# One matmul of 512 columns for the high weights in the feed-forward, its halves added when the bank is emptied

## The reference

```python
def conv_ffn(x, w_gate, w_val, conv_w, conv_b, w_down):
    h = causal_dwconv(x @ w_gate, conv_w) + conv_b     # 3 taps over the tokens
    return (jax.nn.silu(h) * (x @ w_val)) @ w_down

x = layer_norm(ALPHA * x + mixers[layer](x), *ln1[layer])
x = layer_norm(ALPHA * x + conv_ffn(x, *ffns[layer]), *ln2[layer])
```

## Time and profile before

| what | value |
| --- | --- |
| median of 3 runs | 3589.15 us (3586.17 to 3608.59) |
| span of the profiled execution | 3590.3 us, 68886 instructions |
| TensorE busy | 3425.7 us, 95% |
| VectorE busy | 2281.9 us, 64% |
| ScalarE busy | 1603.8 us, 45% |
| read from the chip's memory | 581.31 MB, 162 GB/s over the span |

### The profile page before, as it was taken

One profiled execution on the slowest core, in us unless ns is written; L12 is line 12 of the kernel. 1 busy time (PEld: TensorE's weight loads), 2 busy tenths in 40 slices (PEclk: granted clock), 3 DMA queues, 4 the chain that ended last, 5 costly groups with the idle time before them and its releaser, 6 DMA issues.

```text
span 3590.3 us, 68886 instructions
## 1 busy us (share of the span) xinstructions
PE 3425.7 (95%) x30164; PEld 3358.8 (94%) x30164; DVE 2281.9 (64%) x3711; ACT 1603.8 (45%) x2267; POOL 81.6 (2%) x101
## 2 busy tenths in 40 slices
PE   7899999999998998999999999988998999999997
PEld 7899999999998888899999999987998999999997
DVE  5656556556676678697666655687545976666555
ACT  4544445444445523255444444562433554444443
POOL 0000000000000001000000000002000000000000
PEclk9999999999999989999999999999999999999998
DMA  6455555555454322255555666541443556656664
GB/s 227 146 176 172 169 176 177 174 179 171 159 194 134 106 66 69 82 171 182 194 189 197 196 191 192 188 131 64 166 158 112 169 174 198 195 189 197 193 195 132
DMA packets 162637, 587.88 MB, mean 164 GB/s; under 512 B 18144, under 2 KB 18144, under 8 KB 161952
## 3 DMA queue, kind: packets, MB, share of 16 engines
q1 hardware_dynamic: 160848, 575.06, 49.0%
q0 software_dynamic: 1488, 8.42, 0.7%
HBM read 581.31 MB, written 2.10 MB: 162 GB/s over the span
## 4 chain that ended last, share of the span: by engine, by line
PE 51%; DVE 9%; ACT 1%; issue 1%; POOL 0%; ACTq 0%; DVEq 0%; POOLq 0%
PE bank L1948 15%; PE bank L1950 15%; PE bank L1949 15%; DVE pairs L2691 2%; DVE xs L2807 1%; DVE xs L2805 1%; PE bank L2127 0%; PE bank L1963 0%; PE bank L1964 0%; PE bank L1965 0%; DVE xr L2695 0%; PE bank L2114 0%; DVE xr L2775 0%; DVE right L3133 0%; PE bank L2104 0%
## 5 line engine op out<-in xcount | busy, mean ns | idle before, releaser
L1948 PE MATMUL bank<-xr,pairs 128*128 128x256 f32 (+1 forms) x5920 | 1675.2, 283 | 62.1 <-DVE pairs L2691 50.7
L1949 PE MATMUL bank<-xr,pairs 128*128 128x256 f32 (+1 forms) x5920 | 1650.9, 279 | 0.0
L1950 PE MATMUL bank<-xr,pairs 128*128 128x256 f32 (+1 forms) x5920 | 1650.5, 279 | 0.0
L2380 ACT ACTIVATE pairs<-raw 128x1024 fp32r<-128x1024 f32 x1108 | 1144.4, 1043 | 980.7 <-PE bank L1950 867.0
L2691 DVE TENSOR_TENSOR pairs<-raw,pairs 128x1024 fp32r<-128x1024 f32 x1108 | 1312.8, 1203 | 324.3 <-ACT pairs L2380 321.9
L1948 PEld LDWEIGHTS bank<-xr,pairs 128*128 128x128 f32 x5920 | 1124.0, 190 | 75.9 <-DVE pairs L2691 58.8
L1949 PEld LDWEIGHTS bank<-xr,pairs 128*128 128x128 f32 x5920 | 1123.0, 190 | 1.6
L1950 PEld LDWEIGHTS bank<-xr,pairs 128*128 128x128 f32 x5920 | 1123.5, 190 | 0.0
L1948 PE MATMUL bank<-parts,pairs 128*128 128x256 f32 x1792 | 497.4, 278 | 3.6 <-DVE parts L2695 3.3
L1949 PE MATMUL bank<-parts,pairs 128*128 128x256 f32 x1792 | 495.6, 277 | 0.0
L1950 PE MATMUL bank<-parts,pairs 128*128 128x256 f32 x1792 | 495.6, 277 | 0.0
(11 more groups left out here) (589 smaller groups left out, 3122.4 us busy)
## 6 DMA issues: line engine op xcount, KB each, us to landing
raw<-in_w_in SPq DMA_DIRECT2D x176, 512.0 KB, 4.3
raw<-in_gate SPq DMA_DIRECT2D x176, 512.0 KB, 4.7
raw<-in_val SPq DMA_DIRECT2D x176, 512.0 KB, 4.0
raw<-in_down SPq DMA_DIRECT2D x160, 512.0 KB, 4.5
raw<-in_l_w_in SPq DMA_DIRECT2D x146, 512.0 KB, 3.9
raw<-in_w_out SPq DMA_DIRECT2D x64, 512.0 KB, 4.6
raw<-in_l_w_out SPq DMA_DIRECT2D x64, 512.0 KB, 3.7
raw<-in_v_in SPq DMA_DIRECT2D x48, 512.0 KB, 4.7
```

The lines of the kernel that those rows point to most:

```text
L1948: mm(o, wh[:, q, :], rh[:, k, :], start=begin and q == 0, stop=False)
L1949: mm(o, wh[:, q, :], rl[:, k, :], start=False, stop=False)
L1950: last = mm(o, wl[:, q, :], rh[:, k, :], start=False, stop=end and q == c - 1)
L2380: e.activation(pair_of(n)[0], v3(raw_of(n), widths[n] // slices[n]), ACT.Copy).then_inc(*hi_made(n))
```

## The change

In the 38 tiles of gate and value and in the whole down product of both layers, a product gets a bank of its own. wh x xh and wh x xl become one matmul of 512 columns: `side_by_side` makes an operand of two pieces of 256 columns, high x and low x. Its first half holds wh x xh, its second wh x xl; wl x xh (256 columns) is added into the second. The halves are added when the bank is emptied: for the gate by a copy on ScalarE and an add back into the bank on VectorE, for the value by a copy and an add before the multiplication, and in the down product by a second instruction on x. The first six tiles of each feed-forward, and all other stages, stay as they were.

```diff
+    def side_by_side(hi, lo):
+        return bass.AP(hi.tensor, hi.offset, [hi.ap[0], (lo.offset - hi.offset, 2), *hi.ap[1:]])
...
+    def wide_tile(bk, keys, rhs, ready):
...
+            do("wide", n, bk.view, rhs, k, key is keys[0], key is keys[-1], [ready_at(ready, k + q) for q in range(c)], bk.after)
+            pump()
...
             for j in range(2):
-                m = col_tile(p2[:, j, :], parts(t + j), y, ready, bk)
-            add(bk, t, m)
+                bk = banks.get()
+                m = wide_tile(bk, parts(t + j), y, ready)
+                do("x_add2", sid, bk, t + j, alpha, m, xt[t + j])
+                banks.put(bk, (vec, "x_add", sid, t + j))
+            side.append(norm.step(t, (vec, "x_add", sid, t + 1)))
...
+        def wide_act(t, bk, vbk, gm, m):
...
+            j.b = yield from buf(hb)
+            do("wide_gate", j)
+            do("wide_conv", j)
+            yield
+            j.g = yield from buf(tb)
+            do("ffn_silu", j)
+            banks.put(bk, (vec, "ffn_conv", j.id))
+            yield
+            do("wide_u", j)
...
-                while len(banks.free) < 2:
+                while len(banks.free) < 3:
                     pump()
...
+                bk, vbk = banks.get(), banks.get()
+                gm = wide_tile(bk, both(f"gate{l}", t), X2, last.at)
+                m = wide_tile(vbk, both(f"val{l}", t), X2, last.at)
+            side.append(wide_act(t, bk, vbk, gm, m))
...
+        def wide(n, ps, rhs, k0, begin, end, ready, after):
...
+                mm(ps, wh[:, q, :], side_by_side(rh[:, k, :], rl[:, k, :]), start=begin and q == 0, stop=False)
+                last = mm(ps[:, T:2 * T], wl[:, q, :], rh[:, k, :], start=False, stop=end and q == c - 1)
...
+        def wide_gate(j):
+            w.on(j.b.after)
+            w.on([j.gm])
+            e.activation(j.b.view, j.bk.view[:, T:2 * T], ACT.Copy).then_inc(*act("wide_gate", j.id))
+
+        def wide_u(j):
+            w.on([j.m])
+            w.wait_ge(*act["silu", j.id])
+            e.activation(j.b.view, j.vbk.view[:, T:2 * T], ACT.Copy).then_inc(*act("wide_val", j.id))
...
+        def x_add2(sid, bk, t, alpha, m, xt):
+            w.on([m])
+            w.on(xt)
+            e.scalar_tensor_tensor(out=x[:, t, :], in0=x[:, t, :], scalar=alpha, in1=bk.view[:, 0:T], op0=MUL,
+                                   op1=ADD).then_inc(*vec("x_add0", sid, t))
+            w.wait_ge(*vec.now())
+            e.tensor_tensor(x[:, t, :], x[:, t, :], bk.view[:, T:2 * T], ADD).then_inc(*vec("x_add", sid, t))
...
+        def wide_gate(j):
+            p2 = v3(j.bk.view, 2)
+            w.wait_ge(*act["wide_gate", j.id])
+            e.tensor_tensor(p2[:, 0, :], p2[:, 0, :], j.b.view, ADD).then_inc(*vec("wide_gate", j.id))
...
+        def wide_u(j):
+            p2 = v3(j.vbk.view, 2)
+            w.wait_ge(*act["wide_val", j.id])
+            e.tensor_tensor(j.b.view, j.b.view, p2[:, 0, :], ADD).then_inc(*vec("wide_val", j.id))
+            w.wait_ge(*vec.now())
+            e.tensor_tensor(j.g.view, j.g.view, j.b.view, MUL).then_inc(*vec("ffn_u", j.id))
```

More of the change, by code:

```diff
@@ L543, in col_tile @@
                 pump()
+            k += c
+        return (used, n)
+    def wide_tile(bk, keys, rhs, ready):
+        k = 0
+        for key in keys:
+            n = load(*key)
+            c = widths[n] // 128
+            do("wide", n, bk.view, rhs, k, key is keys[0], key is keys[-1], [ready_at(ready, k + q) for q in range(c)], bk.after)
+            pump()
             k += c
@@ L891, in out_proj @@
         for t in range(4 if first else 0, KT, 2):
-            bk = banks.get()
-            p2 = v3(bk.view, 2)
-            for j in range(2):
-                m = col_tile(p2[:, j, :], parts(t + j), y, ready, bk)
-            add(bk, t, m)
+            if first:
+                bk = banks.get()
+                p2 = v3(bk.view, 2)
+                for j in range(2):
+                    m = col_tile(p2[:, j, :], parts(t + j), y, ready, bk)
+                add(bk, t, m)
+                continue
+            for j in range(2):
+                bk = banks.get()
+                m = wide_tile(bk, parts(t + j), y, ready)
+                do("x_add2", sid, bk, t + j, alpha, m, xt[t + j])
+                banks.put(bk, (vec, "x_add", sid, t + j))
+            side.append(norm.step(t, (vec, "x_add", sid, t + 1)))
         if norm.free is None:
@@ L1565, in act_tile @@
             tb.put(j.g, *ut[t])
+        def wide_act(t, bk, vbk, gm, m):
+            j = Job()
+            j.id, j.l, j.t, j.bk, j.vbk, j.gm, j.m = next(ids), l, t, bk, vbk, gm, m
+            j.b = yield from buf(hb)
[7 more added lines that the diff above has]
+            do("wide_u", j)
+            hb.put(j.b, (vec, "ffn_u", j.id))
+            banks.put(vbk, (vec, "ffn_u", j.id))
+            ut[t] = split(u[0][:, t, :], u[1][:, t, :], j.g.view, (vec, "ffn_u", j.id))
+            tb.put(j.g, *ut[t])
         for t in range(FF):
@@ L1952, in col @@
                 last.then_inc(*used(n))
+        def wide(n, ps, rhs, k0, begin, end, ready, after):
+            (wh, wl), (rh, rl), c = pair_of(n), rhs, widths[n] // 128
+            w.wait_ge(*lo_made[n])
+            if begin:
+                w.on(after)
+            for q in range(c):
+                k = k0 + q
+                w.on(ready[q])
+                mm(ps, wh[:, q, :], side_by_side(rh[:, k, :], rl[:, k, :]), start=begin and q == 0, stop=False)
+                last = mm(ps[:, T:2 * T], wl[:, q, :], rh[:, k, :], start=False, stop=end and q == c - 1)
+            last.then_inc(*used(n))
         def row(n, ps, lhs, k0, ready, after):
@@ L3113, in ffn_conv, with wide_conv @@
                                    op1=ADD).then_inc(*vec("ffn_conv", j.id))
+        def wide_gate(j):
+            p2 = v3(j.bk.view, 2)
+            w.wait_ge(*act["wide_gate", j.id])
+            e.tensor_tensor(p2[:, 0, :], p2[:, 0, :], j.b.view, ADD).then_inc(*vec("wide_gate", j.id))
+        def wide_conv(j):
+            b, p, l, t = j.b.view, j.bk.view, j.l, j.t
+            w.wait_ge(*vec["wide_gate", j.id])
+            e.tensor_scalar(b, p[:, 0:T], VC(f"cw2_{l}", t), VC(f"cb_{l}", t), MUL, ADD).then_inc(*vec("conv2", j.id))
+            w.wait_ge(*vec.now())
+            e.scalar_tensor_tensor(out=b[:, 1:T], in0=p[:, 0:T - 1], scalar=VC(f"cw1_{l}", t), in1=b[:, 1:T], op0=MUL,
+                                   op1=ADD).then_inc(*vec("conv1", j.id))
+            w.wait_ge(*vec.now())
+            e.scalar_tensor_tensor(out=b[:, 2:T], in0=p[:, 0:T - 2], scalar=VC(f"cw0_{l}", t), in1=b[:, 2:T], op0=MUL,
+                                   op1=ADD).then_inc(*vec("ffn_conv", j.id))
+        def wide_u(j):
+            p2 = v3(j.vbk.view, 2)
+            w.wait_ge(*act["wide_val", j.id])
+            e.tensor_tensor(j.b.view, j.b.view, p2[:, 0, :], ADD).then_inc(*vec("wide_val", j.id))
+            w.wait_ge(*vec.now())
+            e.tensor_tensor(j.g.view, j.g.view, j.b.view, MUL).then_inc(*vec("ffn_u", j.id))
         def ffn_gate(j):
@@ L3280, in vector_program @@
                      norm_acc=norm_acc, norm_var=norm_var, norm_R=norm_R, norm_ln=norm_ln, norm_rms=norm_rms, norm_cols=norm_cols, gains=gains, raw_lo=raw_lo,
[L3281 removed]
+                     lead_fix=lead_fix, lead_scale=lead_scale, x_add=x_add, x_add2=x_add2,
                      q_scale=q_scale, k_scale=k_scale, k_copy=k_copy, gate_evict=gate_evict, rope_mm=rope_mm, rope_fin=rope_fin,
```

11 lines of the change are left out of this document (3 added, 8 removed).

## The result

The changed kernel took 3648.97 us (median of 5 runs, 3640.93 to 3651.48), the kernel before 3592.56 us beside it (5 runs, 3586.17 to 3608.59). The ratio on record is 1.0125, 95% interval 1.0085 to 1.0165, so some 1.25% slower, 45 us (the two medians are 56 us apart). That is clear of no change, which was the forecast, and the range ended at 3620 us. The profiled execution took 3642.07 us with a span of 3640.3 us, 50.0 us above that of before.

What follows compares the result with a forecast made beforehand. TensorE's matmul count times start distance was taken as the bound. Span 3590.3 + 0 (matmuls) + 0.5 us (last banks) = 3590.8 us, 3590 us on the median's scale; range 3548 to 3620 us.

Steps and rivals of the forecast that it cites:

- What bounds the kernel: Feed-forward: TensorE waits for nobody, so time is the number of matmuls times the distance between their starts.
- The count: Gate, value and down products, both layers: 3840 matmuls and 3840 weight loads go, no column goes.
- I take 227 ... the term is 3840 x 0 = 0: Merged matmul: 512 columns take 227 ns, as two of 256 did (2 x 113.3), so merging saves 0 us.
- the bound of 230: Upper bound for one 512-column matmul, from the MLA up-projection's value part; at 230 ns the term is +13 us.
- pace lost: Rival, merged groups: 512 columns cost 230 ns and the 256 behind 117.6, group 347.6; +29 us, 3620 us; chance 0.18.
- Load beside it: Rival, merged matmuls: 6.7 ns excess is paid once per instruction, 512 columns take 220 ns; -26 us, 3565; chance 0.17.
- load the limit: Rival, merged matmuls: a weight load hidden behind 512 columns but not 256, 512 takes 215 ns; -45 us, 3546; chance 0.15.
- Emptying the banks at nothing: Gate and value banks: added copies and adds, 0.84 us per tile each on ScalarE and VectorE, run beside TensorE; cost 0.
- The last bank: End of each layer's down product: emptying takes 0.93 us instead of 0.69, together 0.5 us on the path.
- The new stall at even tiles: Down product: VectorE stands until an even tile's last matmul, next weight split queued behind; 0.24 us more fits.

Runs made afterwards that it cites:

- The high weights: Changed kernel with the third matmul multiplying by the high weights, so wl x xh is left out: 3653.13 us (one run).
- the other place of the low x: Changed kernel with the low x 512 bytes further behind the high x (SIDE 256 instead of 128): 3646.23 us (one run).
- the kernel before with that place: Kernel before the change, with the low x 512 bytes further behind the high x: 3589.98 us (one run).
- the merge undone: Changed kernel with each 512-column matmul split again into two of 256, banks and their emptying kept: 3594.23 us, ratio to the kernel before 0.9984.

## Why the prediction was wrong

**What bounds the kernel: right.** Time in this part is the number of matmuls times their distance. TensorE waited for nobody before and after, and the 50.0 us of the span are the 50.0 us of its busy time.

**The count: right.** 3840 matmuls went, and no column.

**"I take 227 ... the term is 3840 x 0 = 0": this step failed.** The reasoning that the excess over 2.4 columns per ns belongs to the columns, not to the instruction, held: 384 and 512 columns carry more of it than 256, and a group of 768 columns took between 340 and 353.3 ns in the mean of every cut and order tried, never less than 340. What was taken wrongly was the pace. The prediction took the fast one for 512 columns (2 x 113.3) from the lower edge of the earlier trace rows and left the third matmul at 113.3. Measured: 235.0 and 118.3, that is 3840 x 13.3 = 51 us in place of 0. The 227 is right for the first merged matmul, which finds the fast pace (225); that a matmul of 512 ends this pace for what follows stood in no term. 235.0 is also above the bound of 230 that was drawn from rows 5: those were nine matmuls in another pattern (512 behind 512 in short rows, which has 226 to 236 here), too few for an edge.

**The rival "pace lost" was the right one in kind, too small in price and chance.** It had 230 + 117.6 = 347.6, 29 us and 0.18; it was 353.3 and 51. Its mechanism was wrong in one point: it laid the pace to where the reads fall in memory. The high weights, the other place of the low x, and the kernel before with that place all left the paces as they were, and the kernel before was at either pace in the same part of two profiles. The earlier trace rows had shown that a second pace exists; that the operand's place made it was only argued.

**The two rivals on the faster side fell.** "Load beside it" wanted 220 ns for 512, "load the limit" 215. Nothing at 512 columns in a merged group was under 225 ns, and with 512 columns, where the load is over in half the time, the excess was more, not less. The Trainium skill, page "TensorE: Matmul & The Clock Gate", section "Wait — 56ns, not 53.3ns?", would have 215.7 ns for 512 columns at the upper clock; no run here shows it for fp32r with a load per matmul: 225 to 236 in the merged groups.

**Emptying the banks at nothing: right.** Shown by the merge undone, 0.9984. VectorE went to 67.7% and 68.5% of the gate and value stretches (71 forecast), ScalarE to 49.0% and 48.2% (55 forecast), both below the forecast: in 100 us there are now fewer tiles, and a copy from a bank takes 0.36 us, not 0.42, which is part of it. The last bank took 0.91 us, 0.93 forecast. The new stall at even tiles cost TensorE nothing: it is busy 100.00 of 100 us in both stretches of the down product.

**What stays open** is why a matmul of 512 switches the pace, and what sets it at a break, where no 512 stands. That the order 512, 256 was at the slow pace 16 times of 16 fits the switching: the way back to the fast pace took three matmuls of 256, and here the next 512 comes after one. This is a reading of the distances, and no run was made for it. Excluded, as far as they were varied, are the place of the low x, the break in the moving operand, which weights are loaded, and the work of the other engines. The last because, within a stretch, the distance behind all 849 matmuls of 512 from 3000 to 3300 us is 234 to 236 ns, while VectorE is busy in some and idle in others. How the pace arises inside TensorE was not tried further.

## What to carry to other kernels

Before merging two matmuls with the same weights, ask whether the time per column or the time per instruction is the limit: compare starts, not durations, of the same format at two widths; if the excess grows with the width, the merge has nothing to give. Where the trace shows two paces for one kind of matmul, price a new pattern at both, and look at its first instructions: they tell whether the pattern found the slow pace or made it. And a pattern of matmuls can be tried cheaply: several orders in one kernel, one after another, give all their distances in one profile.

## What the runs showed of the hardware that was not expected

- fp32r matmuls with a weight load each, at a granted clock of 1.00, ran at 113.3 ns or at 117.8 ns per 256 columns, the same code in the same place, held for 478 us in two profiles: 885 or 851 per 100 us. For one gate and value part that is 18 us; two profiles of the kernel before, one with that part slow, are 12.5 us apart. It may well be part of the kernel's spread, 3587.15 to 3619.80 us over the 13 runs beside the merge undone; that was not shown run by run.
- One matmul of 512 columns among matmuls of 256 switched between the two paces, in either direction, 44 times of 44.
- The distance behind a matmul hangs on the pattern: for 512 columns 225 or 226 ns (first behind 256s at the fast pace), 230 to 236 (further back in a row), 235 (alternating with 256); for 256 columns 113 or 118.
- The number of weight loads did not matter: a third fewer of them (two per group instead of three) gave nothing back. Weight loads were busy 86.9% of a stretch instead of 100%.
- The break in a moving operand of two pieces, whose starts are 16.9 KB apart in the gate and value products, cost nothing: 235.0 ns in one piece and in two.
